# Delta rule of a streaming encoder step: the 16x16 diagonal blocks inverted by forward substitution on VectorE instead of four levels of block products

## The reference, cut to what matters

```python
kb = kc * bc[..., None]
L = jnp.where(strict, jnp.einsum('nbhid,nbhjd->nbhij', kb, kc) * decay, 0.0)
eye = jnp.eye(chunk, dtype=jnp.float32)
rhs = jnp.concatenate([vc * bc[..., None], kb * jnp.exp(G)[..., None]], axis=-1)
sol = lax.linalg.triangular_solve(eye + L, rhs, left_side=True, lower=True)
u, w = sol[..., :DV], sol[..., DV:]
a_qk = jnp.einsum('nbhid,nbhjd->nbhij', qc, kc) * decay
# per chunk: delta = u - w S; o = (q exp(G)) S + a_qk delta; S = S exp(g_last) + (k exp(g_last - G))^T delta
```

## Time and profile before

| what | value |
|---|---|
| median of three runs | 3852.7 us (3850.63 to 3857.19) |
| span of the profiled execution | 3845.6 us |
| TensorE, VectorE, ScalarE, GpSimd busy | 3706.3, 1626.1, 1171.5, 337.2 us |
| first to last chunk's `LT` | 738.7 to 1913.3 us |
| TensorE busy in it | 1105.9 of 1174.6 us |

### The profile page before, as it was taken

One profiled execution on the slowest core, in us unless ns is written; L12 is line 12 of the kernel. 1 busy time (PEld: TensorE's weight loads), 2 busy tenths in 40 slices (PEclk: granted clock), 3 DMA queues, 4 the chain that ended last, 5 costly groups with the idle time before them and its releaser, 6 DMA issues. The chain is left out here.

```text
span 3845.6 us, 53670 instructions
## 1 busy us (share of the span) xinstructions
PE 3706.3 (96%) x20456; PEld 3204.3 (83%) x20456; DVE 1626.1 (42%) x3504; ACT 1171.5 (30%) x2318; POOL 337.2 (9%) x416
## 2 busy tenths in 40 slices
PE   8999999899999999998998999999999999999998
PEld 8999999777777677776667889999999999888886
DVE  4000377655545454544434444444444444432222
ACT  5122222334333333332213333333333333321111
POOL 3000000212111111211200000000000000000000
PEclk9999999899999999999999999999999999999999
DMA  4212322410222212124333331111111111442222
GB/s 156 70 63 65 87 69 70 87 41 24 61 46 46 53 26 48 32 87 144 134 139 105 117 95 46 46 45 45 45 45 45 45 45 48 138 135 82 80 82 67
DMA packets 328015, 278.83 MB, mean 73 GB/s; under 512 B 97106, under 2 KB 292802, under 8 KB 326781
## 3 DMA queue, kind: packets, MB, share of 16 engines
q1 hardware_dynamic: 318207, 258.03, 22.6%
q0 software_dynamic: 5216, 18.23, 1.4%
q10 hardware_dynamic: 4416, 0.14, 0.1%
HBM read 190.70 MB, written 85.65 MB: 72 GB/s over the span
## 5 line engine op out<-in xcount | busy, mean ns | idle before, releaser
L2617 PE MATMUL bank<-ffn_hn_hi,ffn_w_parts 128*128 128x436 f32 (+1 forms) x3520 | 986.4, 361 | 2.2 <-ACTq L2724 2.2
L2617 PEld LDWEIGHTS bank<-ffn_hn_hi,ffn_w_parts 128*128 128x128 f32 x3520 | 661.2, 188 | 38.9 <-issue 2.6
L2617 PE MATMUL bank<-ffn_hn_lo,ffn_w_parts 128*128 128x436 f32 (+1 forms) x1760 | 634.1, 360 | 0.0
L416 PE MATMUL bank<-in_xh,in_wh 128*128 128x436 f32 (+1 forms) x1280 | 357.6, 360 | 2.9 <-DVE in_wh L634 2.9
L2617 PEld LDWEIGHTS bank<-ffn_hn_lo,ffn_w_parts 128*128 128x128 f32 x1760 | 330.8, 188 | 19.3
L2651 PE MATMUL bank<-ffn_down_wa,ffn_g_hi 128*128 (+1 forms) x1224 | 328.9, 391 | 3.9 <-DVE ffn_g_lo L2946 3.9
L2753 ACT COPY ffn_raw<-bank 128x436 f32<-128x436 f32 (+1 forms) x220 | 110.5, 502 | 703.9 <-PE bank L2617 649.4
L1552 PE MATMUL bank<-heads_p_pT,heads_p_v 128*65 128x512 f32 (+3 forms) x640 | 286.4, 529 | 10.3 <-issue 9.8
L2880 DVE TENSOR_SCALAR ffn_hist<-ffn_raw 128x2 f32 (+2 forms) x264 | 45.0, 170 | 546.8 <-ACT ffn_acc L2757 544.0
L2651 PEld LDWEIGHTS bank<-ffn_down_wa,ffn_g_hi 128*128 128x128 f32 x1224 | 230.0, 188 | 53.4 <-DVE ffn_down_wa L2943 3.3
L416 PEld LDWEIGHTS bank<-in_xh,in_wh 128*128 128x128 f32 x1280 | 241.3, 189 | 14.7 <-DVE in_wh L634 3.3
(11 more groups left out here) (418 smaller groups left out, 6369.5 us busy)
## 6 DMA issues: line engine op xcount, KB each, us to landing
ffn_w<-in_w_up_dram SPq DMA_DIRECT2D x44, 512.0 KB, 5.0
ffn_g_raw<-scratch_g SPq DMA_DIRECT2D x110, 192.0 KB, 2.3
scratch_g<-ffn_acc SPq DMA_DIRECT2D x88, 218.0 KB, 2.0
heads_s_k<-in_cache_fox_k_dram SPq DMA_DIRECT2D x8, 2048.0 KB, 13.6
heads_s_v<-in_cache_fox_v_dram SPq DMA_DIRECT2D x8, 2048.0 KB, 8.3
heads_d_qkvT<-scratch_gch SPq DMA_DIRECT2D x17, 768.0 KB, 5.6
ffn_y<-in_w_down_dram SPq DMA_DIRECT2D x22, 512.0 KB, 3.7
scratch_gch<-in_work SPq DMA_DIRECT2D x48, 218.0 KB, 1.9
```

The costliest lines, as they stand in the source:

```text
L416: mm = pe.matmul(bank[:, 4 + i % 2, 0:wide], a[:, k, :], b[:, k, col:col + wide], start=(k == 0 and m == 0), stop=(k == KD - 1 and m == 2))
L2617: mm = pe.matmul(bank[:, pair(n) + e, 0:width], w_parts[a][:, part, e, k, :], x[:, k, cols], start=(k == 0 and m == 0), stop=(k == KD - 1 ...
```

## The change

The levels now begin at `FIRST` = 4. The inverses of the 16x16 diagonal blocks come from forward substitution on VectorE. There are 8 blocks x 4 heads = 32 of them; each gets a partition of its own. SyncE stores the diagonal blocks of `LT` to DRAM with eight DMAs (16 partitions, four heads, runs of 16 floats), loads them back with one DMA as 32 partitions of 256 floats (`l_blk`), VectorE solves in 30 instructions, each behind a wait for the one before, SyncE stores the 32 inverses with one DMA and loads them with eight into the diagonal blocks of `xd`, whose other parts GpSimd has set to zero once. TensorE transposes `xd` and ScalarE copies it to `X`; levels 4 to 6 go on from there. The chunk of the streams uses `xd` directly. The planned time of level 4 is 5 units later than before (42.6 instead of 37.6 behind the start). GpSimd no longer makes `x0` and `XT`, and writes its output into `mixed` in place.

```diff
+    FIRST = 4
+    SOLVED = 41.0
     def level_at(self, t, n):
-        return self.start(t) + 18.0 + self.ROOTS + (n - 1) * 6.0
+        return self.start(t) + self.SOLVED + self.ROOTS + (n - self.FIRST) * 6.0
+    def store_blocks(self, sp, t):
+        s, DS = self.s, self.DS
+        sp.wait_ge(s["lt_ready"], 2 * t + 1)
+        after(sp, s["l_moved"], self.MOVED * t)
+        for b in range(self.NB):
+            at = slice(b * DS, (b + 1) * DS)
+            sp.dma_start(self.io["l_blocks"][b].rearrange("h j i -> j h i"), self.LT[at, :, at]).then_inc(s["l_moved"], 16)
+    def load_blocks(self, sp, t):
+        sp.wait_ge(s["l_moved"], self.MOVED * t + 16 * self.NB)
+        after(sp, s["x_step"], self.SOLVE * t)
+        sp.dma_start(self.l_blk, self.io["l_blocks"].rearrange("b h j i -> (b h) j i")).then_inc(s["l_moved"], 16)
+    def store_inverse(self, sp, t):
+        sp.wait_ge(s["x_step"], self.SOLVE * (t + 1))
+        after(sp, s["x_moved"], self.MOVED * t)
+        sp.dma_start(self.io["x_blocks"].rearrange("b h c i -> (b h) c i"), self.x_blk).then_inc(s["x_moved"], 16)
+    def load_inverse(self, sp, t):
+        sp.wait_ge(s["x_moved"], self.MOVED * t + 16)
...
+        for b in range(self.NB):
+            at = slice(b * DS, (b + 1) * DS)
+            sp.dma_start(self.xd[at, :, at], self.io["x_blocks"][b].rearrange("h c i -> c h i")).then_inc(s["x_moved"], 16)
@@ sync
+            late = self.start(t) + self.ROOTS
+            yield late + 15.2
+            self.store_blocks(sp, t)
+            yield late + 18.0
+            self.load_blocks(sp, t)
             yield self.start(t) + 30.0
...
+            yield late + 34.0
+            self.store_inverse(sp, t)
+            yield late + 36.5
+            self.load_inverse(sp, t)
@@ tensor
-            yield late + 17.6
-            pe.wait_ge(s["lt_ready"], 2 * t + 1)
-            pe.wait_ge(s["xt0_ready"], t + 1)
-            for h in range(GH):
-                mm = pe.transpose(self.at(t, 1, h), self.XT[:, h, :], ident)
-            mm.then_inc(s["x0_mm"], 1)
-            for n in range(1, self.levels(t)):
-                l = self.level_at(t, n)
+            if not self.streams(t):
+                yield late + 39.0
+                pe.wait_ge(s["x_moved"], self.MOVED * (t + 1))
+                for h in range(GH):
+                    mm = pe.transpose(self.at(t, 1, h), self.xd[:, h, :], ident)
+                mm.then_inc(s["xt_mm"], 1)
+            for n in range(self.FIRST, self.levels(t)):
+                l, m = self.level_at(t, n), n - self.FIRST
@@ scalar
-            yield late + 18.6
-            act.wait_ge(s["x0_mm"], t + 1)
-            nc.scalar.copy(self.X[:], self.heads(t, 1)).then_inc(s["x_ready"], 1)
+            if not self.streams(t):
+                yield late + 40.0
+                act.wait_ge(s["xt_mm"], self.LV * t + 1)
+                nc.scalar.copy(self.X[:], self.heads(t, 1)).then_inc(s["x_ready"], 1)
@@ gpsimd
-            pool.wait_ge(s["lt_ready"], 2 * t + 1)
-            nc.gpsimd.tensor_tensor(self.x0[:], self.LT[:], spread(c["level0_t"][:].unsqueeze(1), [P, GH, P]), ALU.mult) \
-                .then_inc(s["pool_x0"], 1)
-            pool.wait_ge(s["pool_x0"], t + 1)
-            nc.gpsimd.tensor_tensor(self.XT[:], self.x0[:], spread(c["ident"][:].unsqueeze(1), [P, GH, P]), ALU.add) \
-                .then_inc(s["xt0_ready"], 1)
@@ vector
+            yield late + 21.0
+            dve.wait_ge(s["l_moved"], self.MOVED * (t + 1))
+            after(dve, s["x_moved"], self.MOVED * t)
+            tt(self.x_blk, self.l_blk, rest, V).then_inc(s["x_step"], 1)
+            dve.wait_ge(s["x_step"], done + 1)
+            diagonal = self.x_blk.rearrange("p c i -> p (c i)")[:, 0:DS * DS:DS + 1]
+            nc.vector.memset(diagonal, 1.0).then_inc(s["x_step"], 1)
+            for j in range(1, DS - 1):
+                yield late + 21.0 + 0.85 * j
+                dve.wait_ge(s["x_step"], done + 2 * j)
+                shape = [c["BLOCKS"], j, DS - 1 - j]
+                some, x = self.outer[:, 0:j, j + 1:], self.x_blk[:, 0:j, j + 1:]
+                tt(some, spread(self.x_blk[:, 0:j, j:j + 1], shape), spread(self.l_blk[:, j:j + 1, j + 1:], shape), V) \
+                    .then_inc(s["x_step"], 1)
+                dve.wait_ge(s["x_step"], done + 2 * j + 1)
+                tt(x, x, some, ALU.subtract).then_inc(s["x_step"], 1)
```

More of the change, by code:

```diff
@@ L99, in make_constants @@
     keep(c["before_q"][:], [[DS, DB], [1, DS]], 0, -1)
-    for n, m in enumerate(c["level"]):
+    for n, m in c["level"].items():
         s = 1 << n
@@ L107, in make_constants @@
         keep(v[:, :, 0, :], [[2 * s, P // (2 * s)], [0, s]], 2 * s - 1, -1)
[L109 to L113, removed]
+    block = c["block_rest"][0:c["BLOCKS"], :].rearrange("p (c i) -> p c i", i=DS)
+    step(nc.gpsimd.memset(block, -1.0))
+    keep(block, [[-1, DS], [1, DS]], -1, 0)
     step(nc.gpsimd.memset(later[:], 1.0))
@@ L810, in __init__ @@
             "qkv_loaded gb_loaded z_loaded small_loaded state_loaded tok_turned gsum_mm decay_mm unitT_mm unitT_out "
-            "kk_mm x0_mm w_mm y_mm xt_mm wt_mm nwt_ready delta_mm delta_ready o_mm s_mm state_ready o_scaled "
+            "kk_mm w_mm y_mm xt_mm wt_mm nwt_ready delta_mm delta_ready o_mm s_mm state_ready o_scaled "
             "gsum_v decay_v decay_ready squares_ready sumsq_ready unit_ready ex_ready fac_v scaled_ready lt_ready "
-            "x_ready w_ready xt0_ready xt_ready xt_last o_sq o_sum o_unit pool_scaled pool_x0 zn_ready mix_ready gnorm_ready "
+            "x_ready w_ready l_moved x_step x_moved xt_ready xt_last o_sq o_sum o_unit pool_scaled zn_ready mix_ready gnorm_ready "
             "mix_stored ex_s_ready streamsT_mm streamsT_ready kdb_ready sb_mm sb_ready s_stored o_out").split()}
@@ L1051, in tensor @@
                 yield l + 3.6
-                pe.wait_ge(s["w_ready"], (self.LEVELS - 1) * t + n)
-                if n == 1:
+                pe.wait_ge(s["w_ready"], self.LV * t + m + 1)
+                if m == 0:
                     pe.wait_ge(s["lt_ready"], 2 * t + 2)
                 else:
-                    pe.wait_ge(s["xt_ready"], (self.LEVELS - 2) * t + n - 1)
-                if n < self.levels(t) - 1:
-                    pairs(t, 2, self.XT, self.wn, "y_mm")
+                    pe.wait_ge(s["xt_ready"], (self.LV - 1) * t + m)
+                if n == self.levels(t) - 1:
+                    pairs(t, 2, self.wn, self.XT, "y_mm")
                 else:
-                    pairs(t, 2, self.wn, self.XT, "y_mm")
+                    pairs(t, 2, self.XT if m else self.xd, self.wn, "y_mm")
             yield self.last_at(t) + 0.8
-            pe.wait_ge(s["xt_last"], t + 1)
+            if self.streams(t):
+                pe.wait_ge(s["x_moved"], self.MOVED * (t + 1))
+                pe.wait_ge(s["unitT_out"], 4 * t + 4)
+            else:
+                pe.wait_ge(s["xt_last"], t + 1)
             pe.wait_ge(s["pool_scaled"], 2 * t + 2)
-            pairs(t, 0, self.kbG, self.XT, "wt_mm")
+            pairs(t, 0, self.kbG, self.xd if self.streams(t) else self.XT, "wt_mm")
             yield from (finish_streams(t) if self.streams(t) else finish(t))
@@ L1220, in vector @@
             dve.wait_ge(s["kk_mm"], 2 * t + 1)
+            after(dve, s["l_moved"], self.MOVED * t)
             tt(self.LT[:], self.heads(t, 1), self.dec[:], V).then_inc(s["lt_ready"], 1)
@@ L1231, in vector @@
                 yield l + 4.8
-                dve.wait_ge(s["y_mm"], (self.LEVELS - 1) * t + n)
+                dve.wait_ge(s["y_mm"], self.LV * t + m + 1)
                 if n < self.levels(t) - 1:
@@ L3075, in sb @@
                     return constants.enter_context(nc.sbuf_tensor(name, shape, F32))
-                for n in ("ones", "tri", "tri_s", "same_stream", "causal", "after", "decay_mask", "decay_mask_s",
-                          "level0_t"):
+                for n in ("ones", "tri", "tri_s", "same_stream", "causal", "after", "decay_mask", "decay_mask_s"):
                     c[n] = sb(n, [P, P])
-                c["level"] = [sb(f"level{n}", [P, P]) for n in range(7)]
+                c["level"] = {n: sb(f"level{n}", [P, P]) for n in range(Delta.FIRST, 7)}
+                c["block_rest"] = sb("block_rest", [P, DS * DS])
                 c["stream_rows"] = sb("stream_rows", [P, DB])
```

58 lines of the change are left out of this document (37 added, 21 removed).

## The result

The changed kernel takes 3887.9 us (median of four runs, 3884.9 to 3893.8); the kernel before takes 3854.9 us beside it (3850.6 to 3863.2). The ratio is 1.009, 95% interval 1.0072 to 1.0107: slower by about 33 us. The forecast was 3971 us, so slower was right, but the loss is 33 us where 118 was forecast; the case that came is rival 2, "near its lower ends", which had a chance of 0.13.

What follows compares the result with a forecast made beforehand. TensorE, busy 96%, was taken as the bound, standing at the new chain's wait. 3845.6 + 50 (sixteen chunks) + 1 (streams' chunk) + 38 (queue) + 29 (clock) = 3964 us, 3971 as a median; low 3870, high 4085.

Steps and rivals of the forecast that it cites:

- rival 2: Whole kernel: same mechanism as the forecast, near its lower ends, 3860 to 3900 us; chance 0.13.
- Freed: TensorE work removed: six product groups and three net transpose groups a chunk, 6.7 us, 17 x 6.7 = 113 us.
- TensorE stands in order at the wait: Before the transposes of `xd`, TensorE waits for `x_moved`; 14 us of attention beside the chain, twelve us without TensorE work.
- The way from `LT` to the transposes: Stores, load, solve, store and loads in sequence: 27.0 us against 25.7 before, +1.3 us a chunk.
- The moves without the queue: Four moves through DRAM a chunk: `store_blocks` 5.9 us, `load_blocks` 2.0, `store_inverse` 1.8, `load_inverse` 5.8.
- The solve: On VectorE: 28 dependent steps, first product and memset 7.2 us, plus attention 3.5 us: 10.7 us a chunk.
- The queue of SyncE: Small DMAs wait for large loads ahead in chunks 0, 5, 10 and 14 to 16: 38 us (10 to 60).
- The rest of the period: Behind the wait: level 4's `w_mm` (0.89), transposes (0.44), copy into `X` (about 0.5): +1.8 us a chunk.
- The clock: TensorE at half clock for one stretch behind each wait for `x_moved`: 17 x 1.7 = 29 us (0 to 58).
- Rival 1: SyncE's eight issues take the time of one: chain 19.4 us, kernel 3849, 3820 without clock loss; chance 0.08 for faster.
- Rival 4: TensorE stays at half clock through the whole stretch: 4043 us, more with slow issues; chance 0.20.
- the marks named ahead: Expected profile signs, such as `LT` period 78 to 79 us; wrong if `LT` to the transposes is under 24 us.

Runs made afterwards that it cites:

- kernel 1: The changed kernel without the four moves and the solve, levels 4 to 6 kept: 3742.4 us, ratio 0.9707 to the kernel before.
- Kernel 11: The changed kernel with ten more dependent VectorE steps of 20 elements behind the solve: 3919.3 us, ratio 1.0165 to the kernel before.
- kernel 9: The changed kernel with the transposes of `xd`, levels 4 to 6 and the finish planned 4 units later: 3835.6 us, ratio 0.995.
- kernel 4: The changed kernel with four groups of dummy TensorE products before the wait for `xd` in the 16 prompt chunks: 3878.4 us, ratio 1.0057.
- kernel 8: The changed kernel with one DMA each way, the next head's loads put behind the moves, and dummy products before the wait: 3841.2 us, ratio 0.9973.
- Kernel 5: The changed kernel with one 256 KB DMA for eight, storing all of `LT` and loading all of `xd`: 3818.4 us, ratio 0.9907.

## Why the direction was right and the size was not

Point by point, in the order of the prediction's sum (profiled executions).

- **Freed: 113 us, measured 107 to 114** (kernel 1). Right.
- **"TensorE stands in order at the wait, so the stretch is as long as its chain": right.** Kernel 11 shows the slope, kernel 9 that the standing comes from the plan: the same chain with 2.4 us more attention before it costs 52 us less. How long it stands was overrated: the prediction had 14 us of work beside the chain and 12 us of standing in each chunk. Kernel 1 has 18.2 us of work there, and the wait is 4.9 us in the mean.
- **The way from `LT` to the transposes, 27.0 us and 35 us of queue in sixteen chunks: this is the step that failed in size.** Together they were 16 x 27.0 + 35 = 467 us; 16 x 25.49 = 408 were measured, 59 us less. By parts:
  - *The moves without the queue: 16.3 us a chunk predicted, 14.2 measured, 33 us in sum, the largest part.* The eight issues take 3.44 and 3.28 us to the last one's start, not 3.8, and what follows them 1.53 and 1.66 us, not 2.1 and 2.0. The landing was taken from transfers of 128 KB with something added for short runs, and 4 KB land in 1.5 to 1.7 us.
  - *The solve: 10.7 us predicted, 9.73 in the mean of all sixteen chunks (8.88 in the undisturbed ones), 15 us in sum.* The steps themselves were priced well: 28 steps of 14 to 56 elements, 0.15 to 0.21 us long and 0.19 to 0.24 us apart, are 6.2 us, with the first product and the memset 6.8 against 7.2. (They have 40 elements on average, not the 20 that the prediction names; its sum counts the right 1120.) The other work of VectorE in between was taken as 3.5 us, its average share of the stage; it is 2.9 in the mean, 2.1 in the undisturbed chunks and 9.7 in chunk 0.
  - *The queue of SyncE: 35 us predicted, about 25 measured, and not where it was put.* Chunk 0 was given 5 us and takes 10.4 (18.0 less the 7.6 of the longer solve); chunk 5 was given 7 and takes 7.2; chunk 10 was given 10 and takes 5.8; chunks 14 and 15 with the 2 MB loads were given 13, and their transposes come at 24.2 and 22.3 us, about the mean. In chunk 0 the eight loads behind the others issue slowly as well, 9.04 us, and only the time to issue the loads in front was counted. Chunk 5 came out as priced; that the sum is only 10 us off is luck, since chunks 0, 10, 14 and 15 did not.
- **The rest of the period: 49.5 us predicted without the clock, 50.26 - 1.5 = 48.8 measured:** 12 us in sum. The term is the +1.8 us a chunk for level 4's product, the transposes and the copy, which comes out as about 1.0; no run says which of the three was too dear.
- **The clock: right.** 29 us predicted, 27 of them for the sixteen periods; 1.5 us a chunk by kernel 4 are 24. The prediction cited the Trainium skill (TensorE: Matmul & The Clock Gate, "The HAM clock gate") on the throttled state, and the rows of chunk 4 agree. That keeping TensorE busy is worth its price is what kernel 8 contradicts here.
- In sum the sixteen periods were put at 50 + 35 + 27 = 112 us more than before, and 37.4 were measured: of the 75 us between, 59 are chain and queue, 12 the rest of the period, 3 the clock. Behind the last `LT` 5.7 us were predicted and 4.3 measured.
- **Rival 1, cheap issue, fell:** an issue costs about 0.45 us. Its remark that the kernel turns faster under about 22 us of chain leaves out the clock: with the prediction's own 38 and 29 us the balance lies near 19.6 (its case at 19.4 gives 3849). Kernel 5, undisturbed at 19.9 us, is faster by 34. The 2.0 us that this rival takes from the Trainium skill (DMA: Bandwidth & Descriptors, "Anatomy of one DMA") stand there for transfers issued by GpSimd, not by SyncE. **Rival 4 fell:** the clock of the stretch is 0.94, not near 0.5.
- **Of the marks named ahead:** period 78 to 79 us (75.75), TensorE's share near 80% (86%), a wait of 4 us or more in each chunk (in nine of sixteen; mean 5.3 over 15, none in chunk 12), VectorE idle 2 to 3 us before the first product (1.8), steps 0.2 us apart (yes), clock under 1 once a chunk (yes). "I am wrong if `LT` to the transposes is under 24 us": it is 23.1 undisturbed, 25.5 over all sixteen.

The error in one line: a chain of six steps, each with a small margin upward, was summed at those margins, and since it repeats sixteen times, chain and queue came out 59 us too long, half of the forecast loss of 118.

## What to carry to other kernels

When an engine in order gives up work for a wait, the time saved is not its work but the wait's: put the chain of one pass, step by step, against the work that the program's order has placed beside it, and multiply by the number of passes. Where that chain goes through memory, count its DMAs before its bytes, and look at what the fixed order of the queue puts ahead of each. And before the change is judged, move the plan: here one large DMA for eight and 4 units of the plan (2.4 us) more attention before the wait turn 0.9% slower into 1.8% faster.

## What the runs showed of the hardware

- Eight DMAs of 4 KB from SyncE take 0.45 us each to issue, also where nothing waits, and land in 1.5 to 1.7 us; one of 256 KB lands in 2.3 (store) or 2.7 us (load). The Trainium skill (DMA: Bandwidth & Descriptors, "Anatomy of one DMA") fits 2.0 us + bytes / 436e3 for transfers issued by GpSimd, an estimate of 2.6 us for 256 KB; the traces of transfers from SyncE lie around it for that size (2.3 and 2.7) and below the 2.0 for the small ones (1.5 to 1.7).
- An issue is not of fixed length. Median and longest of the 136 loads into `xd` are 426 and 5760 ns; behind loads of whole tiles the same instruction holds the queue more than ten times as long.

```profile
L892 SPq DMA_DIRECT2D heads_d_xd<-scratch_x_blocks x136: 315/426/5760, 768.3 to 1976.4; - x136
```

- A dependent VectorE step of 14 elements takes 0.16 us and one of 56 elements 0.20, behind a semaphore each time; ten of 20 elements in a row take 2.0 us. Four times the elements cost 0.04 us more, so in this solve the number of steps counts, hardly their elements.
